# One encoder layer on eight cores: inverse roots on DVE with Newton steps, row sums by one-column matmuls, and streams of their own for the transposes

## The reference

```
h = rmsnorm(x) * g_mix;  z = h @ w_in        # 1024 -> 512 B, 512 C, 512 V, 512 Q, 512 K, 512 Va, 1024 gate_c, 1024 gate_a
y_c = (B * causal_dwconv3(C * V)) @ w_conv_out
Q, K: per 64-wide sub-head rmsnorm, then rotary
per head (4): p_n = softmax(mask(Q_n K_n^T / 8)), n = 0, 1;  o = (p_0 - lam * p_1) @ Va_h
o = rmsnorm(o over its 128 channels) * sub_norm * 0.8;  y_a = o @ w_attn_out
x = x + (sigmoid(gate_c) * y_c + sigmoid(gate_a) * y_a) @ w_o
x = x + (silu(h2 @ w_gate) * (h2 @ w_up)) @ w_down,  h2 = rmsnorm(x) * g_ffn   # 2816 wide
```

## Time and profile before

| | |
|---|---|
| time before, median of 3 runs | 2,713.14 us (2,711.64 to 2,958.53) |
| profiled execution, its time | 2,715.91 us |
| its span (slowest core) | 2,714.3 us |
| instructions | 37,482 |
| PE, DVE, ACT, POOL busy | 2,283.3, 1,615.4, 1,401.1, 319.6 us |
| HBM read, written | 339.45 MB, 66.58 MB |

### The profile page before, as it was taken

How to read it: one execution, slowest core, us unless ns; L and a number is a source line. 1 busy time by engine, 2 the same in 40 slices (tenths; PEclk the granted TensorE clock), 3 DMA queues, 4 the chain that set the end, 5 groups by cost and what they waited for, 6 DMA issues and landing times.

```text
span 2714.3 us, 37482 instructions; the slowest of 8 cores (2697.8 to 2714.3 us)
## 1 busy us (share of the span) xinstructions
PE 2283.3 (84%) x10586; PEld 936.3 (34%) x10800; DVE 1615.4 (60%) x2134; ACT 1401.1 (52%) x2495; POOL 319.6 (12%) x452
## 2 busy tenths in 40 slices
PE   1657688887879988899888998889988899899879
PEld 0213233333324323443233432343333333334334
DVE  3335446535775757457674577856788567885342
ACT  2145326622775626746476565856658466674020
POOL 0330321022003100120002200022000220000000
PEclk9778799988999979999899999999999999999989
DMA  7545774686224343443524444343443334414745
GB/s 181 132 111 122 193 186 138 159 211 210 77 84 139 131 127 134 153 143 126 159 75 148 134 132 148 102 141 123 133 155 102 109 117 144 144 63 125 219 146 175
DMA packets 123066, 376.53 MB, mean 139 GB/s; under 512 B 13552, under 2 KB 15728, under 8 KB 122864
## 3 DMA queue, kind: packets, MB, share of 16 engines
q1 hardware_dynamic: 114080, 342.12, 38.8%
q0 software_dynamic: 8784, 31.99, 7.5%
HBM read 339.45 MB, written 66.58 MB: 150 GB/s over the span
## 4 chain that ended last, share of the span: by engine, by line
PE 61%; ACT 12%; issue 9%; DVE 8%; DMA 5%; POOL 4%; DVEq 0%; ACTq 0%; POOLq 0%; SPq 0%
PE bank L567 37%; PE bank L934 10%; PE bank L813 7%; PE bank L790 4%; ACT Pb L802 3%; ACT L913 1%; DVE Lacc L820 1%; POOL scrP L649 1%; DMA wM<-wblk 1%; POOL scrP L656 1%; ACT scrM L913 1%; DVE yq L658 1%; POOL scrP L653 1%; DMA xs<-x 1%; DMA xr<-xT 1%
## 5 line engine op out<-in xcount | busy, mean ns | idle before, releaser
L802 ACT ACTIVATE Pb<-bank 128x512 bf16<-128x512 f32 (+3 forms) x1152 | 566.3, 566 | 257.3 <-PE bank L790 192.1
L820 DVE TENSOR_TENSOR Lacc<-Lacc,Pb 128x1024 f32<-128x1024 f32 (+3 forms) x544 | 613.7, 1128 | 117.3 <-ACT Pb L802 78.2
L567 PE MATMUL bank<-h,wM 128*128 128x512 bf16 x2756 | 644.3, 384 | 29.5 <-DVE h L901 9.7
L567 PE MATMUL bank<-h,wP 128*128 128x512 bf16 x1749 | 426.9, 390 | 32.9 <-ACT scrP L748 8.5
L567 PEld LDWEIGHTS bank<-h,wM 128*128 128x128 bf16 x2816 | 275.7, 99 | 367.8 <-issue 54.2
L934 PE MATMUL bank<-big,wM 128*128 128x512 bf16 x1374 | 325.6, 380 | 7.5 <-DVE xr L938 3.4
L813 PE MATMUL bank<-Pb,Vs 128*128 128x512 bf16 (+3 forms) x1119 | 309.4, 366 | 18.3 <-POOL Pb L807 7.6
L567 PEld LDWEIGHTS bank<-h,wP 128*128 128x128 bf16 x1792 | 174.8, 100 | 257.8 <-issue 75.8
L915 DVE SCALAR_TENSOR_TENSOR scrM<-scrM,bank 128x512 f32<-128x512 f32 x176 | 120.7, 686 | 230.9 <-ACT scrM L913 202.0
L567 PE MATMUL bank<-wP,h 128*128 128x512 bf16 x749 | 199.7, 417 | 11.4 <-DMA wP<-wblk 6.9
L934 PEld LDWEIGHTS bank<-big,wM 128*128 128x128 bf16 x1408 | 136.4, 98 | 173.4 <-issue 16.6
(11 more groups left out here) (109 smaller groups left out, 2113.4 us busy)
## 6 DMA issues: line engine op xcount, KB each, us to landing
wM<-wsc SPq DMA_DIRECT2D x273, 512.0 KB, 3.7
wP<-wsc SPq DMA_DIRECT2D x154, 512.0 KB, 3.9
wM<-wblk POOLq DMA_DIRECT2D x39, 512.0 KB, 9.4
wsc<-wM SPq DMA_DIRECT2D x39, 512.0 KB, 8.5
xs<-x SPq DMA_DIRECT2D x32, 512.0 KB, 4.0
xr<-xT SPq DMA_DIRECT2D x64, 256.0 KB, 4.5
x1s<-big SPq DMA_DIRECT2D x64, 256.0 KB, 4.3
xr<-x1s SPq DMA_DIRECT2D x64, 256.0 KB, 4.1
```

The source lines that it names most:

```text
L567: ins = nc.tensor.matmul(out(), lhsT=lhs(k), rhs=rhs(k), start=(k == first), stop=(k == last))
L802: pl.op("act", lambda P=P, n=n, N=N, s=st[kt, n]: nc.scalar.activation(out=Pb[:, P.slot[1], n, 0:N], in_=bk(s)[:, 0:N], func=AF.Exp, scale ...
L820: pl.op("dve", lambda P=P, qlo=qlo, N=N: nc.vector.tensor_tensor(out=Lacc[:, :, qlo:T], in0=Lacc[:, :, qlo:T], in1=Pb[:, P.slot[1], :, 0:N ...
```

## The change

- **No Ln.** `rsqrt` computes 1/sqrt(v) with eight small DVE operations: scale and add epsilon, a first guess from the exponent bits (an integer view times -0.5 plus a constant), and two Newton steps. It works on tiles of 1, 4 or 8 columns.
- **Row sums by one-column matmuls.** At the end of a head, lhsT is a block of 128 positions of the split `Lacc`, rhs one column of ones, so that the sums of 128 positions come out on 128 partitions: 16 matmuls for the softmax sums, 4 for the norm. The small result is split into two bf16 parts (`split`, 2 DVE operations), and `spread` brings it back over all partitions: 8 matmuls of 128 columns whose lhsT is the column broadcast and whose rhs is the identity. The head's formula is rearranged: only r = -lam * l0 / l1 is spread, o' = O0 + r * O1, and the factor 1/l0 is taken up by the norm (epsilon times l0 squared).
- **Moved.** The scaling of x rows (L596) and the first part of the split of `Lacc` (L824) go from DVE to ACT, the conv tap L727 and the +1 of gate_a (L766) from DVE to POOL. The first two key tiles of a head are added in one operation from stage 1 on, without the copy L818.
- **Planner.** The banks of the transposes come from streams of their own, N and T, in place of P. Matmul groups of proj whose result goes to a scrP slot now write that slot too ("guards"), so that they are placed only when it is free. `Lacc` additions get priority 6, the small operations 4. The records `cause`, `why` and `freed` change no order.

The diff, cut to its core:

```diff
+        def rsqrt(src, sk, scale, v, y, u, keys, eps=None):
+            kv, ky, ku = keys
+            yi = y.bitcast(I32)
+            vi = v.bitcast(I32)
+            q = [
+                (lambda: nc.vector.tensor_scalar(out=v, in0=src(), scalar1=scale, scalar2=EPS, op0=ALU.mult, op1=ALU.add), [sk], [kv]),
+                (lambda: nc.vector.tensor_scalar(out=yi, in0=vi, scalar1=-0.5, scalar2=float(0x5F1FFFF9), op0=ALU.mult, op1=ALU.add), [kv], [ky]),
+                (lambda: nc.vector.tensor_tensor(out=u, in0=y, in1=y, op=ALU.mult), [ky], [ku]),
+                (lambda: nc.vector.tensor_tensor(out=u, in0=u, in1=v, op=ALU.mult), [ku, kv], [ku]),
+                (lambda: nc.vector.scalar_tensor_tensor(out=y, in0=u, scalar=-2.38924456, in1=y, op0=ALU.add, op1=ALU.mult), [ku, ky], [ky]),
...
+            for f, r, w in q:
+                pl.op("dve", f, r, w, 165, 4)
+
+        def spread(b, pk, n0, ncol, prio, more=()):
+            def fn():
+                ins = None
+                for c in range(ncol):
+                    for p in range(2):
+                        ins = nc.tensor.matmul(bk(b)[:, c * 128:(c + 1) * 128],
+                                               lhsT=hl[:, pk, p, n0 + c:n0 + c + 1].to_broadcast([128, 128]), rhs=ident[:],
+                                               start=(p == 0), stop=(p == 1))
+                return ins
+            pl.op("pe", fn, [("hl", pk), "ident"], [b] + list(more), 2 * ncol * 58.0, prio)
...
-                pl.op("act", lambda ss=ss, sd=sd: nc.scalar.activation(out=sd, in_=ss, func=AF.Ln, bias=EPS, scale=1.0 / D),
...
-                b = pl.tile(F(j), "P")
+                rsqrt(lambda ss=ss: ss, ("ss", t), 1.0 / D, nrm[:, 3, 0, t:t + 1], rs, sd, (("nv", t), ("rs", t), ("sd", t)))
+                pl.op("act", lambda rs=rs: nc.scalar.activation(out=xn[:], in_=xs[:], func=AF.Copy, scale=rs),
+                      ["xs", ("rs", t)], ["xn"], 1060)
+                b = pl.tile(F(j), "N")
...
             def qk_chain(qk, t):
                 b = pl.tile(F(j), "P")
-                tm(H_Q if qk == 0 else H_K, t, b)
                 z, t2 = pl.tile("scrP", "P"), pl.tile("scrP", "P")
+                tm(H_Q if qk == 0 else H_K, t, b, (z, t2))
...
             def qk_fin(qk, t, y):
-                b2 = pl.tile(F(j), "P")
+                b2 = pl.tile(F(j), "T")
...
-                fm(H_CONV + i // 2, (i % 2) * 8, b)
+                nt = pl.tile("scrP", "P") if kind != "b" else None
+                fm(H_CONV + i // 2, (i % 2) * 8, b, () if nt is None else ((nt, "h"), (nt, "m")) if kind == "c" else (nt,))
...
-                pl.op("dve", lambda g=g, dc=dc: nc.vector.tensor_scalar(
+                pl.op("pool", lambda g=g, dc=dc: nc.gpsimd.tensor_scalar(
                     out=gateA[:, dc, :], in0=p_(g)[:, 0:T], scalar1=1.0, scalar2=None, op0=ALU.add),
-                    [g], [("gateA", dc)], DSH)
+                    [g], [("gateA", dc)], 700)
...
-                pl.op("dve", lambda: nc.vector.tensor_copy(LHL[:, 0], Lacc[:]), ["Lacc"], [("LHL", 0)], 700)
+                pl.op("act", lambda: nc.scalar.copy(out=LHL[:, 0], in_=Lacc[:]), ["Lacc"], [("LHL", 0)], 1060)
...
-                for r in rt:
-                    pl.op("act", lambda r=r: nc.scalar.activation(out=a_(r), in_=a_(r), func=AF.Exp, scale=-1.0), [r], [r], A512 + 60)
+                def lsum(lt=lt):
+                    ins = None
+                    for n in range(2):
+                        for c in range(4):
+                            for p in range(2):
+                                ins = nc.tensor.matmul(bk(lt)[:, 4 * n + c:4 * n + c + 1], lhsT=LHL[:, p, n, c * 128:(c + 1) * 128],
+                                                       rhs=ones[:, 0:1], start=(p == 0), stop=(p == 1))
+                    return ins
+                pl.op("pe", lsum, ["ones", ("LHL", 0), ("LHL", 1)], [lt], 16 * 58.0, 0)
...
+                split(nrm[:, 0, 2, 0:4], "rho", 0, 4)
...
+                b = pl.tile(F(j), "A")
+                r0 = pl.tile("scrA", "A")
+                spread(b, 0, 0, 4, 0, [r0])
+                pl.op("act", lambda b=b, r0=r0: nc.scalar.copy(out=a_(r0), in_=bk(b)[:]), [b], [r0], A512)
...
+                rsqrt(lambda b=b: bk(b)[:, 0:4], b, 1.0 / 128, nrm[:, 1, 0, 0:4], nrm[:, 1, 1, 0:4], nrm[:, 1, 2, 0:4],
+                      ("ov", "oy", "ou"), (nrm[:, 0, 1, 4:8], "el0"))
+                split(nrm[:, 1, 1, 0:4], "oy", 1, 4)
+                b = pl.tile(F(j), "A")
+                spread(b, 1, 0, 4, 0, [("onT", h)])
```

More of the change, by code:

```diff
@@ L279, in place @@
             changed = {e}
+            self.why[i] = ("dep", self.cause[i])
+            if unplaced(i):
+                t0, got = slots_for(i)
+                if t0 > est[i]:
+                    sl = max((g[1] for g in got), key=lambda x: slot_free[x])
+                    self.why[i] = ("slot " + str(sl[0]), self.freed.get(sl))
             new = unplaced(i)
@@ L312, in place @@
                     slot_free[t.slot] = t.until + 60.0
+                    self.freed[t.slot] = i
                     changed |= set(free)
@@ L718, in proj @@
                     u = us[c4]
-                    y = pl.tile("scrP", "P")
+                    y = nt
                     us[c4] = y
@@ L780, in attn @@
                     rng = {}
-                    for kt in (g0, g0 + 1):
+                    for kt in range(g0, g0 + QB):
                         r = kt - 4 * j
@@ L825, in attn @@
                 pl.op("dve", lambda: nc.vector.tensor_tensor(out=LHL[:, 1], in0=Lacc[:], in1=LHL[:, 0], op=ALU.subtract),
                       ["Lacc", ("LHL", 0)], [("LHL", 1)], 1220)
-                rt = []
-                for n in range(2):
-                    b = pl.tile(F(j), "A")
-                    def lb(b=b, n=n):
-                        nc.tensor.matmul(bk(b)[:], lhsT=ones[:], rhs=LHL[:, 0, n, :], start=True, stop=False)
-                        return nc.tensor.matmul(bk(b)[:], lhsT=ones[:], rhs=LHL[:, 1, n, :], start=False, stop=True)
-                    pl.op("pe", lb, ["ones", ("LHL", 0), ("LHL", 1)], [b], 2 * PE_N, 0)
-                    r = pl.tile("scrA", "A")
-                    rt.append(r)
-                    pl.op("act", lambda b=b, r=r: nc.scalar.activation(out=a_(r), in_=bk(b)[:], func=AF.Ln), [b], [r], A512)
@@ L852, in attn, with ssum @@
-                pl.op("act", lambda b=b, r1=r1: nc.scalar.activation(out=a_(r1), in_=bk(b)[:], func=AF.Ln, bias=EPS,
-                                                                     scale=1.0 / 128), [b], [r1], A512)
-                pl.op("act", lambda r1=r1: nc.scalar.activation(out=a_(r1), in_=a_(r1), func=AF.Exp, scale=-0.5), [r1], [r1], A512 + 60)
-                pl.op("dve", lambda r0=r0, r1=r1, h=h: nc.vector.scalar_tensor_tensor(
-                    out=onT[:, h, :], in0=a_(r0), scalar=small[:, SM_SN08:SM_SN08 + 1], in1=a_(r1), op0=ALU.mult,
-                    op1=ALU.mult), [r0, r1, "sn08"], [("onT", h)], DS512)
+                def ssum(b=b):
+                    ins = None
+                    for c in range(4):
+                        ins = nc.tensor.matmul(bk(b)[:, c:c + 1], lhsT=sqb[:, c * 128:(c + 1) * 128], rhs=ones[:, 0:1],
+                                               start=True, stop=True)
+                    return ins
@@ L893, in mix, with ssum @@
             b = pl.tile(fp, "M")
-            pl.op("pe", lambda b=b, acc=acc: nc.tensor.matmul(bk(b)[:], lhsT=ones_f[:], rhs=m_(acc), start=True, stop=True),
-                  ["ones_f", acc], [b], 1060, PM)
-            R = pl.tile("scrM", "M")
-            pl.op("act", lambda b=b, R=R: nc.scalar.activation(out=m_(R), in_=bk(b)[:], func=AF.Ln, bias=EPS, scale=1.0 / D),
-                  [b], [R], A512)
-            pl.op("act", lambda R=R: nc.scalar.activation(out=m_(R), in_=m_(R), func=AF.Exp, scale=-0.5), [R], [R], A512 + 60)
+            def ssum(b=b, acc=acc):
+                ins = None
+                for c in range(4):
+                    ins = nc.tensor.matmul(bk(b)[:, c:c + 1], lhsT=m_(acc)[:, c * 128:(c + 1) * 128], rhs=ones_f[:, 0:1],
+                                           start=True, stop=True)
+                return ins
+            pl.op("pe", ssum, ["ones_f", acc], [b], 4 * 400.0, PM)
+            rsqrt(lambda b=b: bk(b)[:, 0:4], b, 1.0 / D, nrm[:, 2, 0, 0:4], nrm[:, 2, 1, 0:4], nrm[:, 2, 2, 0:4],
+                  ("xv", "xy", "xu"))
+            split(nrm[:, 2, 1, 0:4], "xy", 2, 4)
+            R = pl.tile(fp, "M")
+            spread(R, 2, 0, 4, PM)
             for dc in range(8):
                 pl.op("dve", lambda R=R, dc=dc: nc.vector.scalar_tensor_tensor(
-                    out=h2[:, dc, :], in0=x1[:, dc, :], scalar=cst[:, C_GFFN + dc:C_GFFN + dc + 1], in1=m_(R), op0=ALU.mult,
+                    out=h2[:, dc, :], in0=x1[:, dc, :], scalar=cst[:, C_GFFN + dc:C_GFFN + dc + 1], in1=bk(R)[:], op0=ALU.mult,
```

111 lines of the change are left out of this document (71 added, 40 removed).

## The result

The changed kernel takes 2,762.0 us (median; lowest 2,759.3) against 2,712.4 us before: 1.8% slower, ratio 1.0181 with a 95% interval of 1.0161 to 1.0201. The forecast was 2,641 us, the range 2,560 to 2,755; both the side and the range were missed.

The account below looks back on a forecast made before the run. The prediction took PE with its gaps, busy 84% of the span, as the bound. Its terms summed as 2,714 - 47 - 28 - 50 + 15 + 32 + 10 + 10 - 15 = 2,641 us, range 2,560 to 2,755.

Parts of the forecast that it names:

- DVE against POOL, +10 us: Q/K roots on DVE beside POOL's operations: at most 280 us of DVE blocked, 10 us taken, bounds 0 and 140.
- PE's new work: Small matmuls for sums and spreads on PE, less the 160 wide ones removed: net +32 us, from -3 to +85.
- for DVE: Tiny root, split and head operations on DVE: covered except at ends of heads in last stages, +10 us, bounds 0 and 30.
- Ln and Tanh waits: PE's waits for Ln to empty a bank and for a gate's Tanh: -28 us, bounds 0 and 53.
- Q/K chain: PE's 103.2 us of waits for the scaled Q/K rows: -50 us, bounds 0 and 103.
- Standstill: ACT's three waits at L837 for onT, with PE doing mix on one bank: both causes go, -47 us, bounds 0 and 47.
- Q/K waits halved: Sign to look for afterwards: PE's waits for the scaled Q/K rows, 103.2 us before, are halved.
- Guards, +15: Matmul groups wait in PE's queue for the scrP slots of their results: +15 us, bounds 0 and 54.
- rival C: PE pays what it wins, small matmul pairs costing 0.099 us each: 2,694 us, or 2,718 with half the standstills left; chance 0.18.
- rival D: DVE blocked by POOL, half of 280 us reaching PE through FFN and gate banks: 2,771 us; chance 0.14.
- Clock, -15: Granted clock of 0.96 in the middle, 84 us of full-rate work: with less idle time, -15 us, bounds 0 to 40.
- Rival E: Table loads on ACT stay because Tanh, Exp, Square and Copy do not share one table: about 2,709 us; chance 0.04.

Follow-up runs that it names:

- e4: The changed kernel with gateA's plus one and the conv's first tap both back on DVE: 2,642 us, ratio 0.9733 to before.
- e1: The changed kernel with only gateA's plus one back on DVE: 2,678 us, ratio 0.988 to before.
- e3: The changed kernel with gateA still on POOL but the memsets of Pb moved to DVE: 2,682.8 us in one comparable execution.
- e5: The kernel before with gateA's plus one moved to POOL and nothing else: 2,931 us, ratio 1.0813.
- e2: The changed kernel with only the conv's first tap back on DVE: 2,733 us, ratio 1.006 to before.
- e6: The kernel before with Tanh in place of each Ln, same order, inverse-root values left out: 2,558 us, ratio 0.945.
- e16: The kernel before, complete, with new roots only for rows and Q/K, Ln and Exp kept for heads and mix: 2,748 and 2,764 us.
- e14: The kernel before, complete, with new roots only for heads and mix, Ln and Exp kept for rows and Q/K: 2,640 us, ratio 0.971.
- e10: The kernel before with the new end of a head and mix, Tanh in place of Ln for rows and Q/K: 2,595 us, ratio 0.955.
- e15: e4 with no slots asked for ahead of the matmuls and the transposes in the common bank order: 2,648 us, ratio 0.975.
- e11: The kernel before, complete, with all the new inverse roots and nothing else of the change: 2,661 us, ratio 0.980.
- e7: e4 with the low bf16 half left out of row sums and spreads, same order, 544 fewer matmuls: 2,647 us, ratio 0.977.
- e8: e4 with six of eight root instructions per Q/K tile replaced by one-column memsets, same order: 2,634 us, ratio 0.972.
- e9: The kernel before with rows and Q/K roots on DVE, Tanh in place of Ln for heads and mix: 2,636 us, ratio 0.971.
- e13: e9 with six of eight root instructions per Q/K chain replaced by one-column memsets, same order: 2,595 us, ratio 0.953.

## Why the prediction was wrong, point by point

**The step that failed** is the sentence "POOL gets 96 more operations (conv product, gateA)", under *DVE against POOL, +10 us*. I took the moved operations as more of the port's load and left them no term of their own. They measured 120 us (after against e4): 84 to 91 for gateA, 29 to 36 for the tap. The prediction named the order as its greatest risk, but gave it no term and no rival. I knew neither the duration of such an operation on POOL, though one of 128 x 512 at 1.26 us stood in the earlier trace rows, nor what the planner ties to POOL's queue. For a step that is moved to another engine, the question is what stands behind it in the new queue and who waits for that; for gateA the answer was P's corner and with it attention of every stage (e1, e3, e5). For the tap it was simply its 1.56 us, for which the second tap and then PE wait (e2). 2,762 - 120 gives 2,642, within 1 us of the forecast. That is luck: freed alone the loads gave 154 us where two terms held 78, and the roots took back 103 where the terms for PE's new work and for DVE held 52.

**Loads, too small.** The terms *Ln and Tanh waits* (-28) and *Q/K chain* (-50) make 78 us. Freed alone, the loads measured -154 (e6). I had counted only the waits in which PE names ACT. The loads also delay ACT's other work, most where heads and mix keep their Ln (1.1 us a load in e16, 0.36 at rows and Q/K in e14). Of the Q/K term's 50 they gave 27.5 (103.2 to 75.7 in e6).
The Trainium skill, ScalarE: Activation LUTs, section What ACT_TABLE_LOAD costs, adds 1.38 us of drain to each switch. The trace does not show it. These are three rows of ACT before:

```profile
1065.00 0.59 ACT L802 ACTIVATE Pb<-bank 128x512 bf16<-128x512 f32 x1
1065.71 1.28 ACT L852 ACT_TABLE_LOAD   x1
1067.00 0.60 ACT L852 ACTIVATE scrA<-bank 128x512 f32<-128x512 f32 x1
```

The load begins 0.12 us after the end of the operation before it, and the next operation starts 0.01 us after the load.

**Standstill.** Wrong that both causes go. By its letter my sign holds, no ACT wait of over 10 us for onT; but the standstill has another holder. In e4 ACT stands for 29.2, 25.7, 20.5 and 23.6 us, 99 us in all, where a spread of head 1 comes late:

```profile
974.53 1.02 PE L627 MATMUL bank<-onT,wM 128*128 128x512 bf16 x4 [0.51 <-DVE scrM L945]
975.39 0.61 PE L507 MATMUL bank<-ident,hl 128*128 128x128 bf16 x8
...
981.58 0.59 ACT L913 COPY scrA<-bank 128x512 f32<-128x512 f32 x1 [29.16 <-PE bank L507]
```

The first of these L507 is the last spread of head 0, which may come only when mix has read onT; the sums and the first spread of head 1 stand behind it in PE's order. Attention does not cover mix, as I had said it would. What got better is PE in these stretches: busy 86 of 99 us, where before it was 56 of 86. How much of the 47 us that returned was not measured by itself; e10 holds it and the new end of a head together, and comes out at +36 against e6. So the new end costs more than the standstill gave.

**Q/K waits halved.** 19.6 us after, but with 56.8 at L711. Together 76.4, what e6 has without any root at all (75.7). That fits the bound that I had named, POOL's own chain, but no run shortened that chain.

**Guards, +15.** Nothing that shows: without them e4 is 5 us slower and not faster (e15), within the spread. The 56.8 us at L711 are the wait that I had put into PE's queue; in e15 it stands at the transposes again (91.4 us; in e4 29.1 there and 42.0 at L711).

**PE's new work, +32, and rival C.** Sixteen one-column matmuls ran in 0.47 us, 0.03 each and not 0.055:

```profile
248.78 0.48 PEld L897 LDWEIGHTS bank<-ones,LHL 128*128 128x128 bf16 x16 [2.03 <-issue]
248.81 0.54 PE L897 MATMUL bank<-ones,LHL 128*128 128x1 bf16 x16 [1.56 <-DVE LHL L888]
249.28 0.11 PEld L847 LDWEIGHTS bank<-qT,kT 64*128 64x128 bf16 x4
```

PE is busy at most 17 us longer in e11 than before (2,300.0 against 2,283.3), and leaving out half of the small matmuls changes nothing (e7). Rival C is out.

**DVE blocked by POOL, +10, and rival D.** The blocking is there, by the sign that I had set (a mean over 0.4 us in the Q/K chains; it is 0.41). Two of the eight rows of after:

```profile
L491 DVE TENSOR_TENSOR ss<-ss 128x8 f32<-128x8 f32 x64 | 46.5, 726 | 5.3
...
L488 DVE TENSOR_TENSOR ss<-ss 128x8 f32<-128x8 f32 x64 | 16.0, 251 | 5.7 <-DVE ss L487 0.5
```

The eight rows sum to 210 us, 3.3 us a tile where eight undisturbed ones take 1.3. That this is rival D's time would have been the easy story, since 2,771 was its forecast and 2,762 came out. Two things speak against it: the steps take the same 3.3 us a tile in e4, which runs in 2,642 us, and with them shortened there 8 us go (e8). Where no other wait covers them, as in e9, they are worth 41. A right time from a rival does not make it the cause.
The Trainium skill, SBUF — State Buffer, section Who interferes with whom, says that a DVE instruction with two SBUF inputs contends with a GpSimd instruction that reads SBUF, and that the one that issues first has the shared ports for its whole length. The trace agrees: L473 and L475 above end 0.02 us from the end of POOL's, L472 and L474, which start ahead of POOL's, keep their 0.17 us, and the memsets of e8 (no input) keep 59 ns.

**Clock, -15.** In e4 the cores show 0.948 to 0.957, before 0.947 to 0.955. Next to nothing. In after 0.937 to 0.945; its first 400 us run at 0.81 against 0.86 before, but so do those of e1.

**Rival E.** Out: four loads left.

The ledger, from medians:

| step | us | time |
|---|---|---|
| before | | 2,712 |
| no table loads (e6) | -154 | 2,558 |
| roots of rows, Q, K on DVE (e9) | +78 | |
| roots of heads and mix (e10) | +36 | |
| both, complete (e11) | +103 | 2,661 |
| guards, bank order, moved casts and copies, first key tiles added in one, priorities (e4) | -19 | 2,642 |
| tap on POOL (e1) | +36 | 2,678 |
| gateA on POOL (after) | +84 | 2,762 |

Open stays the half of e9's 78 us that e13 leaves (37 us): it lies in the order or in the hand-overs between engines, and no run tells these apart. Which of the remaining edits makes e4 19 us faster than e11 was not tried either; e15 only shows that it is not mostly guards and banks (5 us, within the spread). How far a plan made anew moves the time by itself was not measured, so the steps under 20 us say little.

## What to carry to other kernels

An operation that moves to an idle engine brings that engine's queue with it: before moving, list what else the engine does, in which order it must be done, and who waits for the last of it; here a 0.2 us memset carried the attention of a stage. The same table reload cost 1.1 us each around the Ln of heads and mix and 0.36 us each around rows and Q/K; price stalls by place, not by count. When a standstill is to go, look for who holds it next: here the wait for onT went and the wait for the spread behind it took its place. And split a change whose parts pull both ways: everything else was worth 2.7%, the two moved groups took 4.4%.
